# The triangular inverse of the mixing stage, kept packed by 32-blocks up to step 16, with products in four column groups and operands spread by two engines

## The reference

```python
def step(state, inp):
    r_t, k_t, v_t, w_t, a_t, b_t = inp
    sa = jnp.einsum('bhvk,bhk->bhv', state, a_t)
    state = state * w_t[:, :, None, :] + sa[..., None] * b_t[:, :, None, :] + v_t[..., None] * k_t[:, :, None, :]
    return state, jnp.einsum('bhvk,bhk->bhv', state, r_t)
...
mixed = jnp.concatenate([ret, rw], axis=-1).astype(x.dtype)
h = h + mixed @ w_out[l]
```

## Time and profile before

| what | value |
|---|---|
| median of three runs | 2895.5 us (2890.79 to 2899.98) |
| the profiled execution: its time | 2889.8 us |
| its span, first to last instruction | 2888.0 us |
| mean granted TensorE clock over the span | 0.97 of full |

### The profile page before, as it was taken

One profiled execution on the slowest core, in us unless ns is written; L12 is line 12 of the kernel. 1 busy time (PEld: TensorE's weight loads), 2 busy tenths in 40 slices (PEclk: granted clock), 3 DMA queues, 4 the chain that ended last, 5 costly groups with the idle time before them and its releaser, 6 DMA issues. The chain is left out here.

```text
span 2888.0 us, 38654 instructions
## 1 busy us (share of the span) xinstructions
PE 2693.2 (93%) x14472; PEld 2220.4 (77%) x14473; DVE 1942.9 (67%) x2438; ACT 1350.8 (47%) x1914; POOL 577.5 (20%) x487
## 2 busy tenths in 40 slices
PE   8999988889988879999999699999999899999998
PEld 7988767777776758888888588766677688888887
DVE  4441167777764579999999663586778888887314
ACT  5111155555543257777777452236654334333312
POOL 0000035655550010000000330130000343341000
PEclk9999989999998979999999799999999999999999
DMA  6456111111006459999999631001031222223314
GB/s 205 177 191 251 74 58 54 44 37 36 28 9 232 185 208 408 408 412 409 408 411 368 208 110 47 22 1 60 1 111 63 62 87 87 80 80 116 136 48 160
DMA packets 166286, 439.86 MB, mean 152 GB/s; under 512 B 21852, under 2 KB 102800, under 8 KB 152848
## 3 DMA queue, kind: packets, MB, share of 16 engines
q1 hardware_dynamic: 151552, 384.13, 36.2%
q0 software_dynamic: 8848, 33.03, 3.0%
q10 hardware_dynamic: 5760, 20.97, 1.8%
HBM read 358.93 MB, written 79.17 MB: 152 GB/s over the span
## 5 line engine op out<-in xcount | busy, mean ns | idle before, releaser
L134 PE MATMUL psum<-part,expert_x_high 128*128 128x512 f32 x520 | 207.5, 399 | 2.9 <-issue 1.5
L136 PE MATMUL psum<-part,expert_x_low 128*128 128x512 f32 x520 | 203.8, 392 | 0.0
L134 PE MATMUL psum<-project_w_high,high 128*128 128x448 f32 (+1 forms) x512 | 194.4, 380 | 4.0 <-DVE low L398 4.0
L136 PE MATMUL psum<-project_w_high,low 128*128 128x448 f32 (+1 forms) x512 | 193.5, 378 | 0.0
L135 PE MATMUL psum<-project_w_low,high 128*128 128x448 f32 (+1 forms) x512 | 193.5, 378 | 0.0
L129 DVE TENSOR_TENSOR expert_down_low<-expert_down,expert_down_high 128x2048 fp32r<-128x2048 f32 x62 | 139.3, 2288 | 39.6 <-ACT expert_down_high L124 39.6
L971 POOL TENSOR_TENSOR mix_ab_step<-mix_abrb,mix_pair_mask 128x512 f32<-128x512 f32 x80 | 115.4, 1467 | 182.8 <-ACT mix_abrb L1106 182.4
L129 DVE TENSOR_TENSOR expert_gate_low<-expert_gate,part 128x2048 fp32r<-128x2048 f32 x64 | 143.9, 2289 | 10.0 <-ACT part L124 8.5
L134 PE MATMUL psum<-part,ffn_w_high 128*128 128x512 f32 x352 | 139.9, 397 | 11.4 <-DVE ffn_u L4172 6.3
L129 DVE TENSOR_TENSOR expert_up_low<-expert_up,part 128x2048 fp32r<-128x2048 f32 x64 | 143.8, 2289 | 1.0 <-ACT part L124 1.0
L135 PE MATMUL psum<-ffn_b_low,ffn_w_high 128*128 128x512 f32 x352 | 138.9, 395 | 0.0
(11 more groups left out here) (728 smaller groups left out, 7567.2 us busy)
## 6 DMA issues: line engine op xcount, KB each, us to landing
expert_gate<-in_w_gate_dram SPq DMA_DIRECT2D x32, 2048.0 KB
expert_up<-in_w_up_dram SPq DMA_DIRECT2D x32, 2048.0 KB, 10.2
expert_down<-in_w_down_dram SPq DMA_DIRECT2D x32, 2048.0 KB, 10.9
ffn_w<-in_ffn_w_up_dram SPq DMA_DIRECT2D x44, 512.0 KB, 4.3
y_rows<-expert_y ACTq DMA_DIRECT2D x32, 512.0 KB, 11.0
hidden_rows<-ffn_hidden SPq DMA_DIRECT2D x20, 512.0 KB, 2.8
ffn_hidden<-hidden_rows SPq DMA_DIRECT2D x20, 512.0 KB, 4.1
down_w<-in_ffn_w_down_dram SPq DMA_DIRECT2D x39, 256.0 KB, 2.7
```

The source lines that it names most:

```text
L134: pe.matmul(out, left[0], right[0], start=start, stop=False)
L136: return pe.matmul(out, left[1], right[0], start=False, stop=stop)
```

## The change

The inverse of a 128x128 matrix by blocks of 32 is zero outside its four diagonal 32x32 blocks. The new code keeps only these blocks up to block size 32: 8 heads of 32 columns are 256 columns (`PACKED`) on 128 partitions. DVE copies the diagonal blocks of the scores together (`pk`, eight copies of 32 partitions), one mask each gives the five packed matrices `pb` (the first by DVE, four by POOL, each of 256 columns where an `ab_step` has 512). The inverse grows in PSUM (bank 0) by accumulation, so that DVE's `add_step` is gone.

A matmul of a step has 32 columns of weights and writes 32 partitions, and the four blocks go to four column groups of the array. Its moving operand has to be spread again into blocks on a zeroed 128x128 matrix (`xe`, `ze`). Each spreading is four copies of 32 partitions by 256 columns, two by ACT and two by DVE. For steps 1, 2, 4, 8, 16 there are ten spreadings. The transposed inverse that a step needs as weights (`tf`) comes from two transposes of the packed form. The doublings to 64 and to 128 use small blocks (`half`, `whole`), after one transposition of `xe` to `x_t`. The preparation of the next tile and the fills are the same work, cut in smaller pieces and put in other places; the tail is as before.

```diff
-SOLVE_STEPS = (2, 4, 8, 16, 32, 64)
+LEAF = 32
+PACKED_STEPS = (1, 2, 4, 8, 16)
...
-        ab_step = [[st.sb(f"ab_step{i}_{s}", [P, HG, P]) for s in range(3)] for i in range(2)]
-        x_t, x_n, zs = ([st.sb(f"{n}{i}", [P, HG, P]) for i in range(2)] for n in ("x_t", "x_n", "zs"))
+        pk = st.sb("pk", [P, 2, HG, LEAF])
+        pb = [st.sb(f"pb{s}", [P, 2, HG, LEAF]) for s in range(NP)]
+        nf, tf = st.sb("nf", [P, 2, P]), st.sb("tf", [P, 2, BLOCKS, LEAF])
+        xe, ze, x_t = (st.sb(n, [P, 2, HG, P]) for n in ("xe", "ze", "x_t"))
+        z_half, z_last = st.sb("z_half", [P, 2 * HG, LEAF]), st.sb("z_last", [P, 2 * HG, RW_N])
...
+                    for b in range(BLOCKS):
+                        v.tensor_copy(pk[leaf(b), gr, :, :], two_banks(4 * gr)[leaf(b), :, 0, leaf(b)]).then_inc(ab_packed, 1)
+                v.wait_ge(ab_packed, (t + 1) * 2 * BLOCKS)
+                v.tensor_tensor(every(pb[0]), every(pk), per_block(packed_mask[:, leaf(0)], 2 * HG), ALU.mult).then_inc(pair_ready, 1)
+            def spread_z(t, s):
+                v.wait_ge(z_made, t * NP + s + 1)
+                for b in DVE_BLOCKS:
+                    v.tensor_copy(every(ze)[leaf(b), :, leaf(b)], packed(z_bank(s))[leaf(b)]).then_inc(z_by_dve, 1)
+            def spread_n(t, s):
+                v.wait_ge(n_made, t * NP + s + 1)
+                for b in DVE_BLOCKS:
+                    v.tensor_copy(every(xe)[leaf(b), :, leaf(b)], packed(0)[leaf(b)]).then_inc(n_by_dve, 1)
+            def take_t(t, s):
+                v.wait_ge(n_turned, t * (NP - 1) + s)
+                v.tensor_copy(every(tf), packed(4)).then_inc(t_ready, 1)
+            def take_half(t):
+                v.wait_ge(half_z_made, t + 1)
+                v.tensor_copy(z_half[leaf(3)], packed(1)[leaf(3)]).then_inc(half_by_dve, 1)
+            def place_half(t):
+                v.wait_ge(half_made, t + 1)
+                v.tensor_copy(every(xe)[leaf(1), :, leaf(0)], packed(0)[leaf(1)]).then_inc(placed_by_dve, 1)
+                v.tensor_copy(every(x_t)[leaf(0), :, leaf(1)], packed(0)[leaf(0)]).then_inc(placed_by_dve, 1)
+            def place_last(t):
+                v.wait_ge(last_made, t + 1)
+                v.tensor_copy(every(x_t)[FIRST_HALF, :, SECOND_HALF], three(bank[0][FIRST_HALF, :], 2 * HG)).then_inc(x_last, 1)
+                v.memset(every(xe)[leaf(1), :, leaf(0)], 0.0).then_inc(x_last, 1)
...
+                spread_z(t, 0)
+                if not last:
+                    kk_link = scale_kk(*after)
+                spread_n(t, 0)
+                if not last:
+                    square_kk(kk_link)
+                spread_z(t, 1)
+                take_t(t, 1)
+                scale_state(t, u, first)
+                spread_n(t, 1)
+                if not last:
+                    sigmoid_args(*after)
+                spread_z(t, 2)
+                take_t(t, 2)
+                if not last:
+                    unit_kk(*after, kk_link)
+                spread_n(t, 2)
+                if not last:
+                    divide_kk(kk_link)
+                mask_k(t, 1)
+                spread_z(t, 3)
+                take_t(t, 3)
+                if not last:
+                    rated_link = rated(*after)
+                mask_k(t, 0)
+                spread_n(t, 3)
+                if not last:
+                    rated_k(after[1], rated_link)
+                spread_z(t, 4)
+                take_t(t, 4)
+                if not last:
+                    rated_b(rated_link)
+                spread_n(t, 4)
+                if not first:
+                    rw_link = rw_norm(t - 1)
+                take_half(t)
+                if not first:
+                    rw_divide(t - 1, rw_link)
+                place_half(t)
+                if not last:
+                    tildes_ba(*after)
+                place_last(t)
+                if not last:
+                    tildes_rk(*after)
 ...
+                pool.wait_ge(ab_packed, (t + 1) * 2 * BLOCKS)
+                for s in range(1, NP):
+                    pool.tensor_tensor(every(pb[s]), every(pk), per_block(packed_mask[:, leaf(s)], 2 * HG), ALU.mult)\
+                        .then_inc(steps_ready, 1)
+                for gr in range(2):
+                    pool.wait_ge(ab_ready, t * 2 + gr + 1)
+                    pool.tensor_tensor(abrb[gr][:, :, 1, :], abrb[gr][:, :, 1, :], per_block(strict_incl[:, 1, :], HG),
+                                       ALU.mult).then_inc(rb_masked, 1)
+                rotate(j, u, first)
...
+            def spread_z(t, s):
+                act.wait_ge(z_made, t * NP + s + 1)
+                for b in ACT_BLOCKS:
+                    act.activation(every(ze)[leaf(b), :, leaf(b)], packed(z_bank(s))[leaf(b)], ACT.Copy).then_inc(z_by_act, 1)
+            def spread_n(t, s):
+                act.wait_ge(n_made, t * NP + s + 1)
+                for b in ACT_BLOCKS:
+                    act.activation(every(xe)[leaf(b), :, leaf(b)], packed(0)[leaf(b)], ACT.Copy).then_inc(n_by_act, 1)
+                if s < NP - 1:
+                    act.wait_ge(n_by_dve, (t * NP + s + 1) * len(DVE_BLOCKS))
+                    act.activation(flat(nf[:]), bank[0][:, 0:PACKED], ACT.Copy).then_inc(n_folded, 1)
+            def take_x_t(t):
+                for gr in range(2):
+                    act.wait_ge(x_turned, t * 2 + gr + 1)
+                    act.activation(x_t[:, gr, :, :], three(bank[4 + gr][:], HG), ACT.Copy).then_inc(x_t_ready, 1)
+            def take_half(t):
+                act.wait_ge(half_z_made, t + 1)
+                act.activation(z_half[leaf(1)], packed(1)[leaf(1)], ACT.Copy).then_inc(half_by_act, 1)
+            def place_half(t):
+                act.wait_ge(half_made, t + 1)
+                act.activation(every(x_t)[leaf(2), :, leaf(3)], packed(0)[leaf(2)], ACT.Copy).then_inc(placed_by_act, 1)
+            def take_last_z(t):
+                act.wait_ge(last_z_made, t + 1)
+                act.activation(z_last[SECOND_HALF], three(bank[1][SECOND_HALF, :], 2 * HG), ACT.Copy).then_inc(last_z_ready, 1)
...
+                spread_z(t, 0)
+                if not last:
+                    take_lo(*after)
+                spread_n(t, 0)
+                spread_z(t, 1)
+                if not last:
+                    root_kk(t + 1)
+                spread_n(t, 1)
+                spread_z(t, 2)
+                if not last:
+                    sigmoids(*after)
+                spread_n(t, 2)
+                spread_z(t, 3)
+                if not last:
+                    reach_ends(t + 1, 1 - u)
+                spread_n(t, 3)
+                if not last:
+                    decays(*after)
+                spread_z(t, 4)
+                spread_n(t, 4)
+                if not last:
+                    decay_before(*after)
+                take_x_t(t)
+                take_half(t)
+                if not first:
+                    rw_deviation(t - 1)
+                    act.wait_ge(ret_ready, t - 1)
+                act.wait_ge(ret_in_ready[u], j * 32 + 32)
+                act.activation(gate[u][:], ret_in[u][:, 3 * RET_W:4 * RET_W], ACT.Silu).then_inc(gate_ready, 1)
+                place_half(t)
+                act.wait_ge(q_made, t + 1)
+                act.activation(q_fm[:], two_banks(2)[:, :, 0, :], ACT.Copy).then_inc(q_fm_ready, 1)
+                act.wait_ge(rq_turned, t + 1)
+                act.activation(q_t[:], three(bank[7][:], RET_HEADS), ACT.Copy).then_inc(q_t_ready, 1)
+                take_last_z(t)
+                act.wait_ge(rk_turned, t + 1)
+                act.activation(k_t[:], three(bank[6][:], RET_HEADS), ACT.Copy).then_inc(k_t_ready, 1)
+                act.wait_ge(q_turned, t + 1)
+                act.activation(q1[:], bank[7][:], ACT.Copy).then_inc(q1_ready, 1)
+                if not (isinstance(j, int) and j == PAIRS - 1):
+                    squash(j + 1, u)
...
+            def pair(t):
+                pe.wait_ge(pair_ready, t + 1)
                 for gr in range(2):
+                    last = pe.transpose(bank[z_bank(0)][:, gr * P:(gr + 1) * P], pb[0][:, gr, :, :].rearrange("p h c -> p (h c)"), ident[:])
+                last.then_inc(z_made, 1)
+            def unit(t):
+                pe.wait_ge(ab_ready, t * 2 + 1)
+                for gr in range(2):
+                    for b in range(BLOCKS):
+                        pe.matmul(bank[0][leaf(b), gr * P:(gr + 1) * P], fold[:], ident[:], start=(gr == 0), stop=False,
+                                  skip_group_check=True)
+            def grow(t, s):
+                pe.wait_ge(z_by_act, (t * NP + s + 1) * len(ACT_BLOCKS))
+                pe.wait_ge(z_by_dve, (t * NP + s + 1) * len(DVE_BLOCKS))
+                if s:
+                    pe.wait_ge(t_ready, t * (NP - 1) + s)
+                pe.sem_inc(pe_passed, 1)
+                for gr in range(2):
+                    for b in range(BLOCKS):
```

(96 more changed lines are left out.)

244 lines of the change are left out of this document (64 added, 180 removed).

## The result

The changed kernel takes 2910.65 us (2905.25 to 2913.13), the kernel before 2895.5 on the same chips: a ratio of 1.0051 with a 95% interval of 1.003 to 1.0073, so slower by 15 us. The forecast was 2881. The profiled execution took 2905.25 us with a span of 2903.5, where before had 2889.8 and 2888.0; its mean granted clock is 0.935 against 0.970.

What follows compares the result with a forecast made beforehand. PE was taken as the longest member of the solve's chain, DVE after the change. Solve 42.2, clock 5.6, tail 13.5 and its clock 0.5 made 61.8 us a turn against 63.0; eight turns gave 2881 us, range 2846 to 2912.

Steps and rivals of the forecast that it cites:

- solve at full clock: From DVE's first pack to the inverse's use in `u`: 42.2 us a turn in place of 49.9.
- tail at full clock: Rest of a turn after the solve: mean 13.1 us plus 0.4 because DVE comes later, taken as 13.5.
- clock, solve: Half of the 11.2 us PE streams on the solve's path, lost to the 1.2 GHz level: 5.6 us a turn.
- clock, tail: Extra 0.5 us a turn where the lower clock level lasts into the tail.
- the walk at full clock: Solve after the change, followed along the engines' queues from DVE's pack with PE at 2.4 GHz: 42.2 us.
- rivals 3: It cancels: 5.7 to 7.9 us of the solve's path lost to the clock, no change within 0.3%; chance 0.22.
- rival 4: Clock at 1.2 GHz for all of the solve: 4.4 us more a turn, +35 in all, 2925; chance 0.28.
- my step ends: Forecast times after DVE begins to pack at which steps 0 to 4 and the closing end, in us.
- Rival 5: Four column groups run as two: a narrow product takes 1.04 us, 10 us more in all; no chance given.
- this condition of being wrong: Prediction wrong if a DVE copy of 32 partitions costs more than half of the pair's 0.86 us.
- Rival 1: Clock holds but for one 3.4 us stretch a turn: turn 57.4 us, 45 less in all, 2845; chance 0.22.
- thin use of the array: Argument that narrow products in the solve, filling little of the array, lower PE's clock; set against the 2845 us case.

Runs made afterwards that it cites:

- c2_close: Changed kernel plus idle PE matmuls, two at each place in the solve's steps and six in the closing; 2857.82 us, ratio 0.9873 to the kernel before.
- e2_one_group: c2_close with the growing product of each step writing all to one column group, three quarters of the inverse's growth left out; 2887.18 us, ratio 0.9993.
- a3_narrow2: Changed kernel plus two idle matmuls with 32 columns of weights at each place of the steps; 2866.06 us, ratio 0.989 to the kernel before.
- c1_order: Changed kernel without idle work, step 4 reordered on PE, ACT and DVE (sums, exponentials and second mask later); 2909.73 us, ratio 1.0057.
- e1_close1: c2_close with one idle matmul instead of two at each place of the steps, the closing's six kept; 2866.66 us, ratio 0.9911.

## Why the prediction was wrong

Its sum for a turn was 42.2 + 5.6 + 13.5 + 0.5 = 61.8 us. Measured is 65.5, the mean of six turns, of which 49.0 are solve and 16.5 tail. `c2_close` gives the two parts at full clock: 44.1 for the solve, in the three of its six turns whose solve has a granted clock of 1.00 (44.09, 44.11 and 44.18), and 13.0 for the tail, the mean of six. So term by term:

| term | forecast | measured | from |
| --- | --- | --- | --- |
| solve at full clock | 42.2 | 44.1 | `c2_close`, solves at 1.00 |
| tail at full clock | 13.5 | 13.0 | `c2_close` |
| clock, solve | 5.6 | 4.9 | 49.0 - 44.1 |
| clock, tail | 0.5 | 2.2 | 16.5 - 13.0, less the next |
| stall ahead of L1299 | none | 1.3 | one tail of 23.2 us, 8 longer than its neighbours, over six |

**The mechanism was right for the solve, and two terms of the sum were too small: the walk at full clock, and the clock in the tail.** They are 1.9 and 1.7 of the 3.7 us by which a turn was missed; the other three misses (-0.5, -0.7 and 1.3) nearly cancel. So a forecast gain of 1.2 us a turn became a loss of 2.8 (65.5 against 62.7). The clock falls in the solve and takes back what the shorter chain gives, as the forecast and rivals 3 and 4 had it, and about as long as forecast: with 0.73 granted from 498.15 to 546.07, the lower level held for 0.27 / 0.5 = 54% of that solve, where "about half" was expected. 6.1 us a turn were put down for the clock; 7.1 are measured, and 8.4 with the stall, which the sum did not have. The median shows the clock's share in another way: 2910.65 - 2857.82 = 53 us, 6.6 for each of eight turns, and with the clock held the change gains 35 us over before (2893.25 in that comparison) instead of losing 15.

But the working placed it wrong. It charged 11.2 us of PE on the path, half of it at the lower clock, and 0.5 for a tail with dense work, which lost 2.2. In the trace the third spell begins in the closing and lasts through the densest part of the tail: `u` alone takes 1.6 us more than before. The solve, in which PE waits anyway, lost less than forecast. Half clock costs most where PE is busy, and the spell reaches into that from the waits ahead of it. The rows in hand could have shown this: the stretch from 484 to 488 us at 0.50 was read as a sign of thin work, but `u` begins in it (485.95, 3.51 us), and the tail there is the one of 15.3 us.

**The walk at full clock was 1.9 us short**, the largest single miss of the 3.7 us of a turn; the tail's clock with 1.7 and the stall with 1.3 come next. (That 8 x 3.7 is just 2910.65 - 2881 is chance: the forecast stood on the profiled 2889.8, 5.7 below the median, and the first of the eight turns takes only 55.7 us. The change itself was forecast at 9 us less and measured at 15 more.) Against the turn of `c2_close` that starts at 606.08, my step ends of 6.4, 11.4, 17.2, 22.0, 28.6 and 42.0 stand against 6.9, 12.6, 18.0, 23.2, 30.0 and 44.1:

```profile
612.31 0.65 PE L1348 MATMUL psum<-mix_ze,mix_fold 128*32 128x128 f32 x16 [0.73 <-ACT mix_ze L1152]
...
618.05 0.64 PE L1348 MATMUL psum<-mix_ze,mix_tf 128*32 128x128 f32 x16
...
635.42 0.64 PE L1348 MATMUL psum<-mix_ze,mix_tf 128*32 128x128 f32 x16 [0.42 <-DVE mix_tf L785]
```

No step is far off; nearly each is some tenths longer. The start has measured parts: the packs take 2.51 and not 2.3, POOL's masks 0.9 each and not 0.65. Step 1 adds another 0.7, the closing 0.7. The shape was right: step 4 is long because the sums wait for the mask (5.8 us of waits for L803 in six turns), and `place_half` stands behind the root (DVE waits 2.45 us for ACT). In two of six turns of `c2_close` the solve is 45.8 instead of 44.1. There the clock still falls, during step 4 (0.76 and 0.81 in two stretches of 4 us from 570), and 0.96 is granted over the whole solve. A third solve has 0.96 as well and takes 44.17: its clock falls at the start, from 436 to 440, and costs nothing there.

**Prices.** The narrow product: 0.64 to 0.65, forecast 0.62. Rival 5 falls, by the trace and by `e2_one_group`. The pair of DVE copies 0.88 (0.86), that of ACT 0.77 (0.63, within the bound of 1.0). A copy of 32 partitions with 256 columns takes 0.426 us, so this condition of being wrong did not occur. For the other, a late table load, there is no sign: in the changed kernel from 430 to 830 us PE waits for a spreading copy of ACT five times (7.8 us in all), each time ahead of step 0, and no table load stands in front of that copy.

**Rivals.** The time, slower by 0.5%, falls to what the prediction counted as rival 4, but not by its way: the clock did not stay low for the whole solve, and the rest came from the tail, the stall and the walk. Rival 1, the clock holds as before, gave a turn of 57.4 us and 2845; with idle work that holds it the chip gives 57.7 and 2858, nearly the same turn by misses that cancel (a clock term of 0.6 and not 1.7, a longer walk), and 5.7 of the 13 us are the profiled execution below its median. The Trainium skill, page TensorE: Matmul & The Clock Gate, table under "Why this matters for your kernels", warns of idle gaps longer than any wait for data in this stage. By it the clock would have held; the trace disagrees (0.76, with 2.4 us as the longest such wait). The same page's section "A second HAM failure mode: psum-queue depth-cycling" tells of a PE that idles often and briefly between groups and whose clock swings. With that the trace agrees, and the prediction, which let the page speak for 2845, had passed it over. The reason that I gave against rival 1, thin use of the array, fell with `a3_narrow2`: the right doubt stood on the wrong ground.

The delay at a change of tiling mode, which I left out, is still seen: in `c2_close` the last of the narrow sixteen starts at 635.42 + 0.64 - 0.28 = 635.78, the first of L1428 at 636.00, 0.22 us later. It lies on the path where PE is late, and is part of the tenths above.

## What to carry to other kernels

A change that shortens a chain by taking work off PE can turn PE's busy time into many short waits, and the clock then falls for all that PE does, also for dense work behind the stage; read the granted clock in windows of the tail, not only of the changed part. Before such a change is given up, fill the waits: twenty constant matmuls a turn turned 15 us of loss into 35 us of gain here, while filling of the same kind in a stage bound by PE gave nothing. In the steps 32 columns did as well as 128. Moving single operations off the visible path gave nothing twice: once the work came back on the same queue a few us later, once the tail took back what the solve had gained.

## What the runs showed of the hardware that I had not expected

- Narrow and full idle matmuls hold the clock alike: 2866.06 and 2869.7 us with clocks of 0.93 and 0.91 from 430 to 830 us, where none gives 2910.65 and 0.76.
- The clock stayed at half with PE busy for 8.00 of 8 us (609.74 to 617.74), so a spell that begins among waits is paid for in dense work: 15.3 us for a tail of the kernel before instead of 12.1, 3.5 us for `u` instead of 1.97 in the changed one.
- Column groups of 32: 0.64 us for sixteen matmuls whether neighbouring products lie in the same column group, in pairs, or in different ones, 1.91 us if all lie in one. The Trainium skill, page TensorEngine Tiling (Array Packing), Key Properties, has tiles operate in parallel; these two numbers agree.
- DVE's copies of 32 partitions cost what the columns cost: 0.287 us for 128, 0.426 for 256, and 0.42 for 256 columns on all 128 partitions (L785).
- In the tail of the turn after 611.46, PE waits 4.04 us for nothing that the profile shows, ahead of L1299. A wait of about 2 us at this place is in the traces of both kernels. A longer one is in three traces, of the changed kernel (4.0), `c1_order` (4.2) and `e1_close1` (3.6), and in no other. Its cause stays open.
